# The second token tile's gates, recurrence, merges, glu and output projection, moved behind the first tile's queries

## The reference, cut to what matters

```python
gates = jax.nn.sigmoid(p[..., OFF_G:]).reshape(bsz, seq, N_BRANCH, D_MODEL)
merged = (gates[:, :, 0] * y_a + gates[:, :, 1] * y_b
          + gates[:, :, 2] * y_c + gates[:, :, 3] * y_d)
x = x + gt1 * (merged @ w_o[l])
...
h = rms_norm(x, norm_ffn_g[l]) * (1.0 + sc2) + sh2
x = x + gt2 * (jnp.square(jax.nn.relu(h @ ffn_w1[l])) @ ffn_w2[l])
...
xc, ic, gc = args
u = expert_u[ic]
hval = jnp.einsum('cd,chkd->chk', xc, u).astype(jnp.float32)
a = (gc * jax.nn.gelu(hval, approximate=False)).astype(xc.dtype)
return jnp.einsum('chk,chkd->cd', a, expert_v[ic])
```

## Time and profile before

| | |
|---|---|
| median of three runs | 1557.67 us (1554.61 to 1559.54) |
| profiled execution, its own time | 1565.77 us, span 1564.5 |
| busy: PE, DVE, ACT, POOL | 77%, 63%, 25%, 25% |
| chain that ended last: PE, DMA, DVE | 43%, 26%, 22% |
| moved by DMA | 488.48 MB, mean 312 GB/s |
| granted TensorE clock, mean | 0.888 |

### The profile page before, as it was taken

One profiled execution on the slowest core, in us unless ns is written; L12 is line 12 of the kernel. 1 busy time (PEld: TensorE's weight loads), 2 busy tenths in 40 slices (PEclk: granted clock), 3 DMA queues, 4 the chain that ended last, 5 costly groups with the idle time before them and its releaser, 6 DMA issues.

```text
span 1564.5 us, 13954 instructions
## 1 busy us (share of the span) xinstructions
PE 1204.7 (77%) x4822; PEld 743.9 (48%) x4822; DVE 982.3 (63%) x2054; ACT 389.1 (25%) x1009; POOL 392.5 (25%) x285
## 2 busy tenths in 40 slices
PE   2989999979999799878787466867486666766665
PEld 2875556654767674377555255423282222222222
DVE  6288877844130221156566789768699888888764
ACT  2152112111100222112120332233123433333322
POOL 0001211110000000022333334223256554545530
PEclk9999999969999898988888778879698888889887
DMA  9633433433788564749999989979999999999995
GB/s 373 245 120 121 163 146 135 189 121 148 279 331 338 207 248 183 286 189 424 424 423 423 424 326 420 380 322 361 363 373 415 421 422 421 421 421 422 421 422 218
DMA packets 56231, 488.48 MB, mean 312 GB/s; under 512 B 6496, under 2 KB 8800, under 8 KB 10080
## 3 DMA queue, kind: packets, MB, share of 16 engines
q0 software_dynamic: 36864, 268.45, 41.7%
q1 hardware_dynamic: 18144, 215.55, 35.0%
q10 hardware_dynamic: 1152, 3.59, 0.6%
HBM read 486.51 MB, written 1.05 MB: 312 GB/s over the span
## 4 chain that ended last, share of the span: by engine, by line
PE 43%; DMA 26%; DVE 22%; issue 4%; ACT 3%; POOL 1%; another core or an unknown queue 0%; ACTq 0%; DVEq 0%; SPq 0%
PE ps L416 23%; DMA arena<-in_euv,arena 11%; PE ps L818 7%; DMA ring<-in_w 7%; DMA ring<-in_euv,arena 6%; PE ps L493 6%; PE ps L780 6%; DVE xr L1682 5%; DVE arena L1658 3%; DVE arena L1007 2%; DVE arena L1270 1%; DVE arena L1277 1%; DVE ring L1658 1%; DMA ring<-in_bb 1%; DMA ring<-in_ba 1%
## 5 line engine op out<-in xcount | busy, mean ns | idle before, releaser
L2180 POOL DMA_INDIRECT arena<-in_euv,arena x163 | 223.7, 1373 | 627.9 <-DVE arena L1652 338.2
L416 PE MATMUL ps<-arena,ring 128*128 128x128 f32 (+1 forms) x2320 | 312.8, 298 | 25.8 <-DMA ring<-in_w 5.6
L416 PEld LDWEIGHTS ps<-arena,ring 128*128 128x128 f32 x2320 | 300.1, 201 | 45.8 <-DMA ring<-in_w 7.7
L1658 DVE CUSTOM_DVE_ANT_0 arena<-arena 128x1024 f32<-128x1024 f32 x163 | 197.5, 1222 | 34.8 <-DMA arena<-in_euv,arena 33.6
L946 PE MATMUL ps<-arena 128*128 128x512 f32 x268 | 149.6, 702 | 70.5 <-ACT arena L2083 70.4
L818 PE MATMUL ps<-ring,arena 128*128 128x512 f32 x256 | 129.5, 666 | 33.9 <-DMA ring<-in_w 33.9
L1682 DVE SCALAR_TENSOR_TENSOR xr<-arena,xr 128x1024 f32<-128x1024 f32 x96 | 123.1, 1283 | 36.2 <-ACT arena L2095 31.8
L946 PE MATMUL ps<-ring,arena 128*128 128x512 f32 x164 | 98.7, 746 | 46.6 <-ACT arena L2083 46.6
L946 PEld LDWEIGHTS ps<-arena 128*128 128x128 f32 x268 | 56.3, 221 | 161.4 <-ACT arena L2083 101.1
L416 PE MATMUL ps<-arena 128*128 128x128 f32 (+4 forms) x684 | 117.4, 321 | 20.0 <-ACT arena L1748 16.8
L2180 POOL DMA_INDIRECT ring<-in_euv,arena x74 | 99.7, 1347 | 129.2 <-DVE xr L1682 78.3
(11 more groups left out here) (291 smaller groups left out, 1238.4 us busy)
## 6 DMA issues: line engine op xcount, KB each, us to landing
ring<-in_w SPq DMA_DIRECT2D x32, 2048.0 KB, 8.3
ring<-in_ada SPq DMA_DIRECT2D x12, 2048.0 KB, 12.8
ring<-in_qkv SPq DMA_DIRECT2D x12, 2048.0 KB, 7.6
ring<-in_gates SPq DMA_DIRECT2D x8, 2048.0 KB, 7.4
ring<-in_g SPq DMA_DIRECT2D x8, 2048.0 KB, 7.5
ring<-in_pq SPq DMA_DIRECT2D x8, 2048.0 KB, 7.4
ring<-in_wp SPq DMA_DIRECT2D x5, 2048.0 KB, 7.3
ring<-in_wout SPq DMA_DIRECT2D x4, 2048.0 KB, 7.6
```

The lines of the kernel that those rows point to most:

```text
L416: ins = te.matmul(o, l, r, start=(i == 0), stop=(i == len(pairs) - 1))
L1658: ins = v.tensor_tensor_reduce(out=x, in0=x, in1=xn[:, tt, :], scale=1.0, scalar=0.0, op0=ALU.mult, op1=ALU.add, accum_out=hv[:, n % 16:n ...
L2180: gp.indirect_dma_start(slots[i], None, A["euv"], bass.IndirectOffsetOnAxis(ap=idx[:, n // 16 % 4, e % 16:e % 16 + 1].bitcast(U32), axis=0 ...
```

## The change

Of tile 1, everything behind the input projection except the scans and the preparation of the recurrence is taken out of the first part and put ahead of tile 1's FFN, where picks are woven in:

- `mixer_order` now yields the gates and merges of tile 0 alone, and a shorter `SCHEDULE` with up to four steps behind a half gate. The recurrence is split into a preparation for both tiles and one generator for each tile. Results that tile 1 needs later (masked keys, values, branch outputs, state) get places of their own.
- `tail_units` lists tile 1's 16 half gates, 21 steps of its recurrence (`chain`), merges and glu; `out_units` the output projection (`wo`) and norm (`x0`) of a tile. `last_order` walks `out_units(0)`, `late_units(0)`, and then `tail_units`, `out_units(1)` and `late_units(1)` with `AMONG` = 60 groups among them: 16 before tile 1's FFN, 16 in it, 28 behind.
- The weights of the moved part are loaded twice, once for each tile: 8 gates tiles, three halves of 1 MB (`o_a`, `o_b`, `o_c`), `glu` and two of `w_o`.
- The sums `ada` 6 to 9 leave VectorE for GpSimd, in quarters: for each, 8 TENSOR_SCALAR and 7 TENSOR_TENSOR of [128x512]. `ada` 4 and 5 become a row of 8 matmuls on TensorE (`mod_row`). The level masks of tile 1's recurrence are made by VectorE instead of GpSimd.
- Gathers have 7 places before pick 60 (`JOIN`), 10 to pick 130, then 17. The quarters of a choice are now units of their own (`pick`) and are issued when due.

```diff
-SCHEDULE = ["", "", "", "", "", "", "", "d", "ad", "d", "ad", "da", "d", "db", "d", "bd", "b", "d", "bcd", "bcd",
...
-PLAN = [("gates", 4), ("ada", 4), ("gates", 5), ("gates", 2), ("ada", 5), ("gates", 3), ("bc", 0), ("gates", 6),
...
+SCHEDULE = ["", "", "", "", "", "", "", "d", "ad", "d", "ad", "da", "d", "db", "d", "bd", "b", "d", "bcad", "bcda",
...
+GATES = ((4, 5, 2, 3, 0, 1, 6, 7), (4, 5, 2, 3, 6, 7, 0, 1))
...
-        elif kind == "gates":
-            for tt in range(2):
-                for part in range(2):
-                    yield "gate", (i, tt, part)
-                    yield from (("step", (s,)) for s in next(steps))
...
+        yield "gate", (GATES[0][j // 2], j % 2)
+        yield from (("step", (s,)) for s in next(steps))
+        if stage < 2:
+            yield "ada", (i, 2 * stage)
+            yield "ada", (i, 2 * stage + 1)
+        if stage == 2:
+            yield "mod", (i,)
...
+            yield "merge", ((2, 1)[j // 4],)
+            yield "row", (4 + j // 4,)
+            yield from (("step", (s,)) for s in next(steps))
+            yield "mod", (4 + j // 4,)
...
+def tail_units():
+    chain = [(("chain", i), 1) for i in range(21)]
+    for n, g in enumerate(GATES[1]):
+        for part in range(2):
+            yield ("mgate", g, part), 4
+            if chain:
+                yield chain.pop(0)
+            if chain and n % 2:
+                yield chain.pop(0)
+        if n == 1:
+            yield from ((("merge", 2, hf), 1) for hf in range(2))
+        if n == 3:
+            yield from ((("merge", 1, hf), 1) for hf in range(2))
+        if n == 5:
+            yield from ((("glu", hf), 2) for hf in range(2))
+    yield from chain
+    yield from ((("merge", 0, hf), 1) for hf in range(2))
+
+
+
+def out_units(tt):
+    if tt == 0:
+        yield from ((("glu", hf), 2) for hf in range(2))
+    yield from (((("zT",), 1), (("wo", 0), 7), (("wo", 1), 7), (("x0", 0), 3), (("x0", 1), 3)))
...
-    for kind, i in PLAN:
-        names += [(kind, i)] if kind != "bc" else [("o_ab", 0), ("o_c", 0)]
-    names += [("ada", 8), ("o_ab", 1), ("ada", 9), ("glu", 0), ("w_o", 0), ("w_o", 1)]
...
+    names += [("gates", 4, 0), ("ada", 6), ("gates", 5, 0), ("o_c", 0, 0), ("ada", 4), ("gates", 2, 0), ("ada", 7),
+              ("gates", 3, 0), ("o_b", 0, 0), ("ada", 5), ("gates", 0, 0), ("ada", 8), ("gates", 1, 0),
+              ("gates", 6, 0), ("ada", 9), ("gates", 7, 0), ("o_a", 0, 0), ("glu", 0, 0)]
     for tt in range(2):
-        names += [("w1", 0, tt)]
+        if tt:
+            for n, g in enumerate(GATES[1]):
+                names += [("gates", g, 1)] + ([(("o_c", "o_b", "glu", "o_a")[n // 2], 0, 1)] if n % 2 else [])
+        names += [("w_o", 0, tt), ("w_o", 1, tt), ("w1", 0, tt)]
...
-SECOND = PLACE[("w1", 0, 1)]
+SECOND = PLACE[("gates", GATES[1][0], 1)]
...
-AMONG = 52
+AMONG = 60
+
+JOIN = 60
...
-    for u, _ in late_units(0):
-        if u != ("fT",):
-            yield u, 0
-    units = list(late_units(1))
+
+    for u, _ in [*out_units(0), *late_units(0)]:
+        yield u, 0
+    units = [*tail_units(), *out_units(1), *late_units(1)]
...
+    def group(g):
+        step, k = divmod(g, PER_STEP)
+        if k == 0 and step + 2 < len(STEPS):
+            due.extend((step + 2, q) for q in range(4))
+        weigh = None
+        if due and (due[0][0] < 8 or scored) and (k % 2 == 0 or len(due) > 4 - k // 2):
+            s, q = due.pop(0)
+            yield ("pick", s, q), None
+            weigh = s if q == 3 else None
+        yield ("group", g), None
+        if weigh is not None:
+            yield ("weigh", weigh), None
...
+        def slot_at(o):
+            return arena[:, o:o + 2 * D]
+
+        assert slot_top <= ARENA - D
+        slots = [slot_at(o) for o in range(slot_top, ARENA - 3 * D + 1, 2 * D)]
+        slots += [slot_at(0), ring[:, 2, 0:2 * D], ring[:, 2, 2 * D:4 * D], slot_at(ARENA - D)]
+        n_first = len(slots)
+
+        slots += [slot_at(late_top), slot_at(late_top + 2 * D), K[:, K_SU:K_SU + 2 * D]]
         n_early = len(slots)
         slots += [ring[:, r, j * 2 * D:(j + 1) * 2 * D] for r in range(2) for j in range(2)]
         slots += [f4(pexp), keys, kT2.rearrange("p a b c -> p (a b c)")]
-        slot_of, turn_of = row_slots(range(n_early), {2 * AMONG + 10: list(range(n_early, len(slots)))})
+        slot_of, turn_of = row_slots(range(n_first), {JOIN: list(range(n_first, n_early)),
+                                                      2 * AMONG + 10: list(range(n_early, len(slots)))})
...
+            def mod_row(i):
+
+                w, o = weights("ada", i), take(f"mod{i}", "misc")
+                te.wait_ge(*loaded("ada", i))
+                mm(o[:], [(cact[:, k:k + 1].broadcast_to([P, P]), w[:, k * 512:(k + 1) * 512])
+                          for k in range(8)]).then_inc(*fill(f"mod{i}"))
+                spent[("ada", i)] = full(f"mod{i}")
 
...
-                        v.wait_ge(sig("Mo"), 6)
-                        v.wait_ge(*full("St"))
-                    masked(f"MT{tt}", MT, su)
-                    masked(f"Mak{tt}", Mak, su)
-                    masked(f"Mrb{tt}", Mrb, iu)
-                    masked(f"Mrk{tt}", Mrk, iu)
+                def level(i):
+
+                    return v.tensor_tensor(Mo[i % 2], MT, bc4(K[:, K_LEV + i * 128:K_LEV + (i + 1) * 128]), ALU.mult)
+
+                if tt:
...
+            def ada_sum(i, q):
+
+                w, acc = weights("ada", i), mrow[:, i % 2, :]
+                part = (junk[:, 0:512], junk[:, 512:1024])
+                if q == 0:
+                    gp.wait_ge(*loaded("ada", i))
+                    gp.wait_ge(*full(f"mod{i - (4 if i < 8 else 2)}"))
+                for k in (2 * q, 2 * q + 1):
+                    if ada_ops[0]:
+                        gp.wait_ge(sig("pool_ada"), ada_ops[0])
+                    ada_ops[0] += 1
+                    gp.tensor_scalar(part[k % 2] if k else acc, w[:, k * 512:(k + 1) * 512], cact[:, k:k + 1], None,
+                                     ALU.mult).then_inc(sig("pool_ada"), 1)
+                for k in (2 * q, 2 * q + 1):
+                    if k:
+                        gp.wait_ge(sig("pool_ada"), ada_ops[0])
+                        ada_ops[0] += 1
+                        gp.tensor_tensor(acc, acc, part[k % 2], ALU.add).then_inc(sig("pool_ada"), 1)
...
                     gp.wait_ge(sig("chosen"), n // 16 + 1)
                 if i in last:
                     gp.wait_ge(*slot_done[last[i]])
+                elif i < n_first:
+                    gp.wait_ge(*full("sc0.3" if i == n_first - 1 else "sc0.0"))
+                    gp.wait_ge(*spent[STREAM[[m for m in range(SECOND) if SPOT[m] == 2][-1]]])
                 elif i < n_early:
-                    gp.wait_ge(*full("sc0.3" if i == n_early - 1 else "sc0.0"))
```

## The result

The changed kernel takes 1625.8 us, median of four runs (1623.7 to 1633.4), where the kernel before took 1557.95 beside it: a ratio of 1.0447, 95% interval 1.0409 to 1.0486. It is 4.5% slower. I had said 1567.7 us, 0.6% slower, with a range up to 1600: the direction was right, the size was not, and the range missed it.

The account below looks back on a forecast made before the run. Time was taken as the gathers' start, set by TensorE's chain, plus bytes behind it at 422 GB/s, DMA losses and the end. 1565.8 - 64 + 62 + 12 = 1575.8 us profiled, 1567.7 against the median; range 1532 to 1600.

Parts of the forecast that it names:

- The start: Work ahead of the first gather: first stretch ends at 295, FFN starts at 337, gathers at 626, 64 us earlier.
- Rival A: First stretch: VectorE never waits, it ends at 272, the start gains 87 us; 1538 us in all, chance 0.39.
- Rival C: First stretch: each of 60 GpSimd instructions stops VectorE for its whole 1.09 us; 1607 us in all, chance 0.06.
- The prediction's other figure: GpSimd's sums in the first stretch: some 0.44 us for a TENSOR_SCALAR, from the skill; shown by no run then.
- The bytes: Behind the first gather: tile 1's second weight loads, 26.2 MB, cost 62 us at 422 GB/s by displacing picks.
- the third term: Behind the first gather: what the DMA engines lose, 12 us more than before, bounds -10 and +45.
- The losses: Moved part: DMA needs 142 us, VectorE level at 138; one norm loses 9 us, tile 1's attention 3 us.
- the prediction's own sign of being wrong: First stretch ending before 280 or behind 315, or the woven part losing more than 20 us beyond the former 45.
- Rival B: Moved part: VectorE and the recurrence's round trips set 165 us where DMA needs 142; 1591 us in all, chance 0.13.
- The seven places: Gathers before pick 60: seven places instead of ten still hold 17 us of transfers at full rate, costing nothing.
- The attention: Tile 1's attention, 28 groups instead of 33: shrinks by 25 us or loses them; taken as 3 us lost.
- The bytes moved in all: Whole kernel: 515 MB moved, given as one of the signs that would show the forecast's steps.

Follow-up runs that it names:

- the copy's order: Changed kernel with ScalarE's share of a group of picks behind its copy of the recurrence's next step instead of ahead of it: 1616.7 us, ratio 1.0375.
- the four rounds left out: Changed kernel with tile 1's matrix inverse stopped after two of six rounds, so its output is not the reference's: 1605.0 us, ratio 1.0289.

## Why the prediction was wrong, step by step

**The start: the mechanism right, the size 11 us off.** Said: first stretch to 295, FFN at 337, first gather at 626. Measured: 303, 349.3 and 636.6. The 4 us that were to be gained between FFN and first gather are 5. VectorE's own work and the collisions were well priced: its busy time was to be 106 + 27 = 133 us and was 133.5; the collisions, 27 us by 0.45 a piece, measure 23, some 0.39 for each of 60. Mis-sized was the term of waiting, 164 - 133.5 = 30.5 us instead of 23, and the tail to the FFN took 46 us instead of 42. GpSimd's TENSOR_SCALAR, which I priced like a TENSOR_TENSOR at 1.09 us, took 1.77 on average, 32 times, its TENSOR_TENSOR 1.31, so a sum is 23 us of GpSimd; it began late, by 31 us in all for its loads, and TensorE stood 22 us for two of them. Rival A's 272 us, a stretch without waiting, was reached in no run; the nearest, with the sums on VectorE, ends near 290. With the sums on VectorE the stretches come out where I had put them with the sums on GpSimd: FFN at 336.6, first gather at 624.7. Rival C, the port that stops VectorE for a whole instruction, is refuted as a price by the same rows: 0.39 us a piece where it needed 1.09. The rule of the Trainium skill (SBUF — State Buffer, "SBUF: two separate sides") stands then for the collision and not for its full length as a price. The prediction's other figure, some 0.44 us for a TENSOR_SCALAR, is an estimate worked out from the 1.03 cycles an element at 1.2 GHz of the Trainium skill (GPSIMD Engine Reference, "Elementwise — side-by-side cycle accounting"). The trace does not bear it out: the shortest of the 32 took 1.56 us. All ran beside a busy VectorE, so how much of that is collision is not shown (minimum, median and maximum in ns; then its additions by line, 139 to 349):

```profile
L2284 POOL TENSOR_SCALAR arena<-ring,cact x32: 1562/1794/2156, 114.0 to 291.9; 128x512 f32<-128x512 f32 x32
```

```profile
L2290 POOL TENSOR_TENSOR arena<-arena 128x512 f32<-128x512 f32 x25 | 32.7, 1310 | 2.0
```

**The bytes: the failing step in thought.** The sum said: 26.2 MB more behind the first gather, 62 us. As arithmetic it holds only if the DMA engines stay full, and the third term then asks for what they lose. I priced both separately. The run with small loads shows that they aren't two costs: with 22.5 MB less the kernel is as long, since the engines' idle time grows by what the bytes shrink.

**The losses: the failing step in number.** Said: the moved part is bound by data, 142 us, VectorE level with it at 138, so 12 us are lost over the 45 of before, 45 more at worst. Measured: 183 us from the first half gate, and 49 us lost beyond the bytes (58 + 53 - 62); 204 x (1 - 334/422) = 43 of them lie between 637 and 841. It is the prediction's own sign of being wrong, more than 20 us. Two things are missing in that step. First, I never added up TensorE for the moved part, though the rows were there: 16 half gates of 3.44 us, 55, 14 of projection and 20 matmuls of merges and glu at 0.87, 17, and the recurrence, 28 in the run without picks. It is 115 us at full clock, alone, and 131 with picks. VectorE measures 123 us there, not 138, and the data 183 x 329/422 = 143 us. Second, I took the largest of the loads for the length. The data wasn't what set it, since with 53 us less of it A stayed. Two engines with 131 and 123 us of work, which wait in order for each other and for ScalarE, made 183 us, both under three quarters busy. The prediction saw that VectorE and DMA were level and drew only rival B from it, 165 us.

**Rival B** named the right place, and its sign came (334 GB/s in the part on average, under its 390), but it was 18 us short of 183, I gave it 0.13, and its condition, VectorE's load past 142 us, was not met: that load was 123. The run with the recurrence first shows that the round trips are not slow in themselves; without picks the part takes 128 us, and the copy's order (11 to 14 us of A) and the four rounds left out (17 to 20 us) fit a cost of sharing ScalarE's and VectorE's queues with picks.

**The seven places,** costed at nothing, cost nothing, in both kernels. **The attention** was to shrink by 25 us with fewer picks, or to lose them. Up to the last queries (885 to 1165 before, 1016 to 1265 now) it shrank from 280 to 249 us and lost 39 us of data instead of 38, so here the forecast held. B, which holds it, shrank by 63 us for the 80 us of picks' data taken out of it, 4.0 us a group. The runs with 24 and 11 groups show how this goes on: at that point a group taken out of B returns 2.5 us, half of its data's 5. **The bytes moved in all** were to be 515 MB and are 512.6; the end behind the last transfers 14 us, and is 13.

**What stays open.** Of the 54 us that 16 groups add to the part, 12 to 16 are TensorE's busy time at a lower clock, some 19 more waiting for VectorE, 9 for ScalarE, 2 for weights and 8 without a releaser in the profile. The order on ScalarE gave 11 to 14 us back, but 3 to 7 of these are TensorE's busy time, so it is not a further term of this sum. No run took the waits for VectorE away. A part of ScalarE's may be this: in the moved part ScalarE alternates between sigmoid (gates, L1958) and gelu (picks, L2235), and each change loads a table. ScalarE in order of time:

```profile
699.31 1.28 ACT L1958 ACT_TABLE_LOAD   x1 [2.84 <-PE ps L606]
700.60 0.60 ACT L1958 ACTIVATE arena<-ps 128x512 f32<-128x512 f32 x1
701.22 1.28 ACT L2235 ACT_TABLE_LOAD   x1
702.51 0.20 ACT L2235 ACTIVATE arena<-arena 128x2 f32<-128x2 f32 x1
702.75 0.48 ACT L2238 ACTIVATE arena<-arena 128x1 f32<-128x1 f32 x2
```

There are 25 such loads in A, 32 us of ScalarE, against 4 without picks; in the chain those at L1958 and L2235 are 2.6% of 637 to 841, 5 us. The Trainium skill (ScalarE: Activation LUTs, "Table sets: the hidden batching unit") asks for calls batched by table set, which the weaving of gates with picks breaks; the trace agrees that each change is a load. No run took the loads away alone, so their share is argued and not shown; the run with ScalarE's copy first has the same 25 and is shorter, the one with the recurrence first has 19 and is longer, so they don't set A's order.

## What to carry to other kernels

Before work is moved behind a stage that is bound by data, add up every engine for it, TensorE first, and not only the bytes it brings along: the moved part here is 115 us of TensorE, and taking 22.5 of its 26 MB away gained nothing that showed. Where two engines that wait for each other in order have nearly equal sums, the stage can be much longer than the larger of them; here 131 us of TensorE and 123 of VectorE made 183. And a unit woven in costs in each stage something else (4 to 5 us in the moved part, 2.5 in FFN and attention, its data's 5 alone), so how many go where is worth a run for each side: fewer in the tightest stage gained 1%.

## What the hardware showed that I had not expected

- A TENSOR_SCALAR of 128x512 on GpSimd took 1.77 us on average beside a dense VectorE (1.56 to 2.16), more than a TENSOR_TENSOR's 1.31 of the same size in the same stretch.
- Where picks were woven between TensorE's matmuls, its granted clock was lower: 1.00 (2.4 GHz all through) over the 128 us without picks, in which it was 89% busy, 0.85 (partly 1.2 GHz) over the 183 us with them, in which it was 72% busy; the half gates' matmul averages 597 and 653 ns.
- A load of ScalarE's table takes 1.28 us, and a stretch that alternates sigmoid and gelu has 25 of them in 200 us. In the rows above the switch cost no more than that: the next instruction began 0.01 us behind the load.
